# 28 of the 32 up blocks of each squared-ReLU layer as 14 pairs, each pair in seven products of half width

## The chip, the cores and the metric

The kernel runs on one core of a Trainium2 chip. The metric is the device time of one execution in microseconds, as the median of several runs. The engines of the core are PE (matrix products; its weight loads have a line of their own, PEld), DVE and ACT (elementwise work), POOL (elementwise work and transfers of its own queue) and SP (which issues most transfers). Each works through its own queue in order, and they wait for each other on semaphores.

## The reference

A transformer of two blocks on 512 tokens of 1024 features, in float32. First block: stick-breaking attention, a squared-ReLU layer, retention, a second squared-ReLU layer. Second block: a SwiGLU layer, a mixed attention and mLSTM layer, another SwiGLU layer. The change touches the two squared-ReLU layers:

```
def squared_relu_mlp(h, w_up, w_down):      # w_up 1024 x 4096, w_down 4096 x 1024
    u = jax.nn.relu(h @ w_up)
    return (u * u) @ w_down

h = h + squared_relu_mlp(rms_norm(h, g_mlp[layer]), w_mlp_up[layer], w_mlp_down[layer])
```

## The kernel before

Features lie on the 128 partitions and the T = 512 tokens along them. A product of full precision is built of three products of a shorter type (`fp32r`): with w = w_hi + w_lo and x = x_hi + x_lo it sums w_hi·x_hi, w_hi·x_lo and w_lo·x_hi in PSUM. A **block** is 128 output features from 1024 input features: `dense` (lines 2051 to 2065) issues 3 x 8 = 24 matmuls of 512 columns, each with its weight load.

Around every block there is the same small production line, two blocks ahead of PE: SP loads 512 KB of weights into `raw` (L466), ACT rounds them to `w_hi` (L578, 128x1024), DVE takes the rest as `w_lo` (L1197). Both halves have two slots.

A squared-ReLU layer has 32 up blocks and 32 down blocks, in groups of 8 (`groups`, one copy for each engine). The order is ups of group 0, ups of group 1, downs of group 0, ups of group 2, downs of group 1, and so on, so that 8 ups lie between the making of a group's hidden values and their use; `u_hi` and `u_lo` have two buffers for that. After an up block DVE forms relu(product) times the norm's reciprocal `inv` (L1209, `u_act`), ACT squares it (L757) and rounds it (L745, `u_hi`), DVE takes the rest (L1427, `u_lo`). After a down block DVE adds the product to the residual `h` in one operation (L1377). The ups' and downs' repetitions are loops on each engine (L206).

At a norm (`ahead_of_norm`, `residual_of_norm`, `of_new_x`) each chunk of the residual is added by DVE, rounded to `x_hi` by ACT (L593) and its rest `x_lo` taken by DVE (L1224), while POOL adds up squares (L2019, L2022); PE starts the next block chunk by chunk (L2099, L2102).

## Time and profile before

| | before |
|---|---|
| median of 3 runs | 2479.38 us (2479.18 to 2479.76) |
| profiled execution, span from first to last instruction | 2477.6 us |
| PE busy | 2469.6 us, 100% |
| DVE busy | 1384.1 us, 56% |
| ACT busy | 952.4 us, 38% |
| POOL busy | 104.0 us, 4% |
| DMA engines | 29.5% of their time, 91 GB/s on average |
| granted clock of PE | 1.00 throughout |

Times inside the kernel are microseconds from the span's start. A matmul's own duration in a row overlaps that of its neighbours; what a matmul costs in a stream is the distance between starts. The idle time in brackets behind a row is that of its engine just before it, with what ended it.

### The profile page before, as it was taken

The page shows a single profiled execution, that of the slowest core. Times are in us where ns is not written, and L with a number is a line of the kernel's source. Part 1 is how long each engine was busy: PE and PEld are TensorE (multiplying, and loading weights), DVE is VectorE, ACT ScalarE, POOL GpSimd, SP SyncE. Part 2 cuts the span into 40 slices and gives each one's busy share as a digit, 9 for nine tenths or more (in the row PEclk, how much of TensorE's full clock was granted, in tenths as well). Part 3 has the DMA queues.
Part 4 walks back from the last instruction along what each step waited for, and adds up shares of the span by engine and source line. Part 5 has one row for each costly group of instructions (what it writes and reads, how often), then busy time and mean ns, then how long its engine had stood idle before and what let it go on. Part 6 is the DMA issues. An engine that isn't in the chain of part 4 may idle for free.

```text
span 2477.6 us, 31594 instructions
## 1 busy us (share of the span) xinstructions
PE 2469.6 (100%) x11544; PEld 2029.9 (82%) x11544; DVE 1384.1 (56%) x1762; ACT 952.4 (38%) x1213; POOL 104.0 (4%) x83
## 2 busy tenths in 40 slices
PE   9999999999999999999999999999999999999999
PEld 7888888888888888888888888888777778888887
DVE  5777544344767765544344544545868846544343
ACT  3676433233334343442233323223465453333222
POOL 2000100001000000100002100001000001000000
PEclk9999999999999999999999999999999999999999
DMA  4112332233222222333333232333222223333333
GB/s 140 57 52 60 94 101 93 96 109 109 85 85 77 77 85 85 104 98 93 101 94 95 93 101 93 98 98 110 85 69 69 77 64 98 93 97 98 93 101 111
DMA packets 76061, 225.40 MB, mean 91 GB/s; under 512 B 12240, under 2 KB 22736, under 8 KB 75856
## 3 DMA queue, kind: packets, MB, share of 16 engines
q1 hardware_dynamic: 71744, 222.24, 29.5%
q10 hardware_dynamic: 4240, 2.10, 0.3%
q8 instruction: 52, 0.85, 0.1%
q14 instruction: 25, 0.20, 0.0%
HBM read 222.21 MB, written 2.10 MB: 91 GB/s over the span
## 4 chain that ended last, share of the span: by engine, by line
PE 97%; DVE 2%; issue 0%; DMA 0%; ACT 0%; ACTq 0%; SPq 0%; DVEq 0%
PE ps L2060 54%; PE ps L2065 27%; PE ps L2667 2%; PE ps L2129 2%; PE ps L2113 1%; PE ps L2410 1%; PE ps L2285 1%; PE ps L2242 1%; PE ps L2261 1%; PE ps L2226 1%; PE ps L2397 1%; PE ps L2248 1%; DVE score L1799 1%; PE ps L2644 0%; PE ps L2722 0%; PE ps L2274 0%
## 5 line engine op out<-in xcount | busy, mean ns | idle before, releaser
L578 ACT ACTIVATE w_hi<-raw 128x1024 fp32r<-128x1024 f32 x406 | 430.7, 1061 | 1204.0 <-PE ps L2065 1155.1
L2060 PE MATMUL ps<-x_hi,w_hi 128*128 128x512 f32 x1936 | 761.7, 393 | 0.0
L2060 PE MATMUL ps<-x_lo,w_hi 128*128 128x512 f32 x1936 | 754.0, 389 | 0.0
L1197 DVE TENSOR_TENSOR w_lo<-raw,w_hi 128x1024 fp32r<-128x1024 f32 x406 | 499.8, 1231 | 150.3 <-ACT w_hi L578 150.0
L2065 PE MATMUL ps<-x_hi,w_lo 128*128 128x512 f32 x1936 | 478.2, 389 | 0.0
L2060 PEld LDWEIGHTS ps<-x_hi,w_hi 128*128 128x128 f32 x1936 | 363.5, 188 | 80.6 <-issue 4.0
L2060 PEld LDWEIGHTS ps<-x_lo,w_hi 128*128 128x128 f32 x1936 | 363.6, 188 | 75.5 <-issue 1.7
L2065 PEld LDWEIGHTS ps<-x_hi,w_lo 128*128 128x128 f32 x1936 | 363.4, 188 | 75.6
L2060 PE MATMUL ps<-u_hi,w_hi 128*128 128x512 f32 x858 | 334.3, 390 | 0.0
L2060 PE MATMUL ps<-u_lo,w_hi 128*128 128x512 f32 x858 | 333.9, 389 | 0.0
L1377 DVE SCALAR_TENSOR_TENSOR h<-ps,h 128x512 f32 (+1 forms) x135 | 93.3, 691 | 337.6 <-PE ps L2065 333.3
L2065 PE MATMUL ps<-u_hi,w_lo 128*128 128x512 f32 x858 | 212.5, 389 | 0.0
L2065 PEld LDWEIGHTS ps<-u_hi,w_lo 128*128 128x128 f32 x858 | 161.0, 188 | 33.5
L2060 PEld LDWEIGHTS ps<-u_hi,w_hi 128*128 128x128 f32 x858 | 161.1, 188 | 33.4
L2060 PEld LDWEIGHTS ps<-u_lo,w_hi 128*128 128x128 f32 x858 | 161.0, 188 | 33.3
L1209 DVE SCALAR_TENSOR_TENSOR u_act<-ps,inv 128x512 f32<-128x512 f32 x108 | 74.6, 691 | 168.4 <-PE ps L2065 168.2
L1427 DVE TENSOR_TENSOR u_lo<-u,u_hi 128x512 f32 (+1 forms) x108 | 74.8, 693 | 59.0 <-ACT u_hi L745 59.0
L745 ACT ACTIVATE u_hi<-u 128x512 f32 (+1 forms) x108 | 68.3, 633 | 95.8 <-DVE u L1459 87.5
L1209 DVE SCALAR_TENSOR_TENSOR u<-ps,inv 128x512 f32<-128x512 f32 x44 | 30.4, 691 | 130.7 <-PE ps L2065 130.7
L2022 POOL TENSOR_TENSOR rstd<-rstd,xn 128x512 f32<-128x512 f32 x49 | 81.2, 1657 | 137.1 <-ACT xn L599 118.4
L2019 POOL COPY rstd<-xn 128x512 f32<-128x512 f32 x7 | 4.8, 688 | 1694.4 <-ACT xn L599 1384.7
L1224 DVE SCALAR_TENSOR_TENSOR x_lo<-h,prm,x_hi 128x512 fp32r<-128x512 f32 x48 | 48.5, 1018 | 4.4 <-ACT x_hi L593 4.2
(386 smaller groups left out, 2438.7 us busy)
## 6 DMA issues: line engine op xcount, KB each, us to landing
raw<-in_stream SPq DMA_DIRECT2D x413, 512.0 KB, 3.6
x_tok<-in_x SPq DMA_DIRECT2D x4, 512.0 KB, 7.8
out_x<-xn ACTq DMA_DIRECT2D x7, 256.0 KB, 2.3
tab_ret<-in_tables_ret SPq DMA_DIRECT2D x1, 1536.0 KB, 6.5
raw<-in_stream SPq DMA_DIRECT2D x3, 256.0 KB, 3.2
tab_mix<-in_tables_mix SPq DMA_DIRECT2D x1, 384.0 KB, 4.2
prm<-in_params SPq DMA_DIRECT2D x1, 298.5 KB, 4.7
out_x<-xn ACTq DMA_DIRECT2D x2, 128.0 KB, 1.8
```

The source lines that it names most:

```text
L578: nc.scalar.activation(w_hi[:, slot(n)], raw[:, slot(n)], ACT.Copy).then_inc(hi_done, 1)
L745: nc.scalar.activation(flat(u_hi[:, group % 2, at(t, scale, plus)]), u[:, plus], ACT.Copy).then_inc(sig("uh_done"), 1)
L1197: nc.vector.tensor_tensor(w_lo[:, slot(n)], raw[:, slot(n)], w_hi[:, slot(n)].bitcast(F32), ALU.subtract).then_inc(lo_done, 1)
L1209: nc.vector.scalar_tensor_tensor(out=dst, in0=product(n), scalar=scale, in1=inv[:], op0=op, op1=ALU.mult).then_inc(bank_free[slot(n)], 1)
L1224: nc.vector.scalar_tensor_tensor(out=x_lo[:, c], in0=h[:, c], scalar=gain, in1=x_hi[:, c].bitcast(F32), op0=ALU.mult, op1=ALU.subtract).th ...
L1377: nc.vector.scalar_tensor_tensor(out=dst, in0=product(n), scalar=scale, in1=dst, op0=ALU.mult, op1=ALU.add).then_inc(bank_free[slot(n)], 1)
L1427: nc.vector.tensor_tensor(flat(u_lo[:, group % 2, at(t, scale, plus)]), u[:, plus], flat(u_hi[:, group % 2, at(t, scale, plus)]).bitcast(F32),
L2022: nc.gpsimd.tensor_tensor(total[:], total[:], square, ALU.add).then_inc(sig("sum_done"), 1)
L2060: nc.tensor.matmul(ps[:, gemm_bank(n)], w_hi[:, s, k], x(k), start=(k == 0 and i == 0), stop=False)
L2065: last = nc.tensor.matmul(ps[:, gemm_bank(n)], w_lo[:, s, k], hi(k), start=False, stop=(k == kc - 1))
L2129: return nc.tensor.matmul(ps[:, VALUE_BANKS[g][tb]], x[:, c, tb * P:(tb + 1) * P], w[:, slot(n), PAIRS * k:PAIRS * (k + 1)].rearrange("p i ...
L2667: last = nc.tensor.matmul(ps[:, bank], w[:, slot(n), 4 * half + k], x[:, k], start=(k == 0 and i == 0), stop=(k == 3 and i == 2))
```

## The change

Four up blocks of each layer stay as they were. The other 28 are taken as 14 pairs. For a pair, the 256 x 1024 weights are a 2 x 2 arrangement of quarters (128 outputs x 512 inputs) and the input is a 2 x 2 arrangement (512 features x 256 tokens). In place of 8 quarter products, 7 products are computed, of sums of quarters on both sides (Winograd's form of Strassen's scheme, by which several products add up in one PSUM bank). One product, called a unit, is 12 matmuls of 256 columns: 4 chunks by 3 terms. A pair has 84 of them, where it had 48 of 512 columns.

New work around it. The sums of inputs (`xs_hi`, `xs_lo`) are made once for each layer at its norm. Of the weights, five of the seven forms lie in `forms`, which has two buffers, one for each pair in turn: SP loads three transfers (512, 512 and 256 KB) and POOL then issues a transfer of 512 KB that adds to what lies there; DVE adds up the other two (`form_sum`). ACT rounds each form (`form_high`), DVE takes the rest (`form_low`), in rings of four. The sums of products are read out of PSUM in halves: ACT copies two (`first_copy`, `second_copy`) between two units that add to the same bank, DVE one (`third_copy`), and DVE forms three sums. ACT then does relu, square and rounding as separate operations. The layer's norm factor is left out of the up blocks; its square `inv_sq` multiplies the down products, which thus take DVE two operations (`down_product`).

The order of the layer changes as well: 4 dense blocks and pairs 0 and 1, downs of group 0, pairs 2 to 5, downs of group 1, and so on. Each group's downs follow directly on its own ups, and the hidden values have one buffer, since the forms take the place of the other.

In the diff, `load_forms` is SP's, `add_forms` POOL's, the first loop over `v` ACT's, the second DVE's and `of_new_u` PE's.

```diff
+def up_phase(layer, g):
...
+    units = [(qs[0], p) for p in (1, 2, 6, 5, 7)]
+    for q in qs[1:]:
+        units += [(q, 1), (q - 1, 4), (q - 1, 3), (q, 2), (q, 6), (q, 5), (q, 7)]
+    return units + [(qs[-1], 4), (qs[-1], 3)]
...
+            def load_forms(q):
...
+                if q % UP_PAIRS < 2:
+                    sp.wait_ge(mm_done, RUN_AT[("mlp0", "mlp1")[q // UP_PAIRS]] + 2 + 1)
+                else:
+                    sp.wait_ge(*upto("f_lo", UNIT_AT[q - 2, 3] + 1))
+                into = forms[q % 2]
+                sp.dma_start(into[:, 0:2].rearrange("p a f -> p (a f)"), stream[block]).then_inc(flag(f"r_in_{q % 2}"), 16)
+                sp.dma_start(into[:, 3:5].rearrange("p a f -> p (a f)"), stream[block + 1]).then_inc(flag(f"r_in_{q % 2}"), 16)
+                sp.dma_start(into[:, 2], stream[block, :, 0:T]).then_inc(flag(f"r_in_{q % 2}"), 16)
...
+            def add_forms(q):
...
+                pool.wait_ge(*upto(f"r_in_{q % 2}", 48 * (q // 2 + 1)))
+                nc.gpsimd.dma_start(forms[q % 2][:, 2:4].rearrange("p a f -> p (a f)"), stream[up_block_at(q) + 1],
+                                    accum_op=ALU.add).then_inc(sig(f"added_{q % 2}"), 16)
...
+                for v in range(first, first + len(units)):
...
+                    if before and before[1] in (1, 6):
+                        copy_of(*before)
+                    if v + 3 < end:
+                        form_high(v + 3)
+                    if q > qs[0] and p == 6:
+                        squared(q - 1, 0)
...
+                for v in range(first, first + len(units)):
...
+                    if before[1] == 7:
+                        fourth_sum(layer, before[0])
...
+                    if p == 4 and q + 1 < (layer + 1) * UP_PAIRS:
+                        third_form(q + 1)
+                    if v + 2 < end:
+                        form_low(v + 2)
+                    if p == 3 and q + 1 < (layer + 1) * UP_PAIRS:
+                        fourth_form(q + 1)
+                    if p == 4 and q > qs[0]:
+                        up_low(layer, q - 1, 0)
+                    if p == 7 and q > qs[0] + 1:
+                        up_low(layer, q - 2, 1)
+                if len(qs) > 1:
+                    up_low(layer, qs[-2], 1)
+                third_sum(qs[-1])
+                up_low(layer, qs[-1], 0)
+                up_low(layer, qs[-1], 1)
...
+            def of_new_u(n, made):
...
+                for chunks in (range(KC - 2), (KC - 2,), (KC - 1,)):
+                    pe.wait_ge(sig("ul_done"), made + chunks[-1] + 1)
```

On PE, at the end of a group's ups and the start of the downs that follow, the queue of before reads (loop bodies; `ul_done` counts the hidden chunks that are ready):

```order
L2065 MATMUL ps<-x_hi,w_lo 128x512 [waits lo_done]
L2065 MATMUL ps<-x_hi,w_lo 128x512 x7
L206 REGISTER_ALU
L206 COMPARE_AND_BRANCH
L206 UNCONDITIONAL_BRANCH [waits ul_done]
L206 ISA
L2051 REGISTER_ALU [waits hi_done]
L2060 MATMUL ps<-u_hi,w_hi 128x512 [waits bank_free_0]
```

And now (`sph_done` and `spl_done` count the rounded forms and their rests, `su_done` DVE's operations on products):

```order
L2820 MATMUL ps<-xs_hi,ring 128x256 [waits su_done,sph_done]
...
L2824 MATMUL ps<-xs_hi,ring_b 128x256 [waits spl_done]
L2824 MATMUL ps<-xs_hi,ring_b 128x256 x3
L2837 MATMUL ps<-u_hi,w_hi 128x512 [waits lo_done,ul_done,bank_free_0,hi_done]
L2837 MATMUL ps<-u_hi,w_hi 128x512 x5
L2837 MATMUL ps<-u_lo,w_hi 128x512 x6
L2837 MATMUL ps<-u_hi,w_lo 128x512 x6
L2837 MATMUL ps<-u_hi,w_hi 128x512 [waits ul_done]
```

The downs now wait for chunks of the units just before them, the first 18 matmuls for chunks 0 to 5 together; before, they waited for chunks made 8 blocks earlier.

On DVE, at the end of a group's ups, the queue of before is this loop body and then the downs':

```order
L1209 SCALAR_TENSOR_TENSOR u_act<-ps,inv 128x512 [waits mm_done]
L1197 TENSOR_TENSOR w_lo<-raw,w_hi 128x1024 [waits hi_done]
L1426 REGISTER_ALU
L1427 ISA [waits uh_done]
L1427 TENSOR_TENSOR u_lo<-u,u_hi 128x512
L206 REGISTER_ALU
L206 COMPARE_AND_BRANCH
L206 UNCONDITIONAL_BRANCH
L206 ISA
L1377 ISA [waits mm_done]
L1377 SCALAR_TENSOR_TENSOR h<-ps,h 128x512
```

And now, from the end of unit 7 of the group's last pair (`third_copy` is `fourth_sum`'s first half, L1740 and L1745 are the third and fourth form of the next group's first pair, `added_0` the adding transfer, L1783 the hidden values' rests):

```order
L1768 COPY third_copy<-ps 128x256 [waits cum_done,su_done]
L1770 TENSOR_TENSOR u<-ps,third_copy 128x256 [waits cum_done,su_done]
L1740 TENSOR_TENSOR form_sum<-forms_80 128x512 [waits x_in_2,added_0]
L1733 TENSOR_TENSOR ring_b<-forms_80,ring 128x512 [waits sph_done]
L1783 TENSOR_TENSOR u_lo<-u_act,u_hi 128x512 [waits uh_done]
L1733 TENSOR_TENSOR ring_b<-forms_80,ring 128x512 [waits sph_done]
L1745 TENSOR_TENSOR form_sum<-forms_80,form_sum 128x512 [waits sp_done]
L1783 TENSOR_TENSOR u_lo<-inv_final,u_hi 128x512 [waits uh_done]
L1776 TENSOR_TENSOR u<-ps,second_copy 128x256 [waits cum_done,exp_done]
L1783 TENSOR_TENSOR u_lo<-u,u_hi 128x512 [waits uh_done] x2
L1681 TENSOR_TENSOR down<-ps,inv_sq 128x512 [waits mm_done,qkl_done]
```

The rest of chunk 5 (the second L1783 row), for which PE's first down matmul waits, now stands behind four operations on the next pair's weights, one of which waits for a transfer.

On ACT, in the middle of a group, the queue had for each up block these rows:

```order
L578 ACTIVATE w_hi<-raw 128x1024 [waits mm_done]
L757 ACTIVATE u<-u_act 128x512 [waits bank_free_0]
L744 REGISTER_ALU
L745 ISA [waits u_done]
L745 ACTIVATE u_hi<-u 128x512
```

And now, where the next pair but one is first read (`x_in_2` counts SP's three transfers into `forms`, buffer 0):

```order
L911 ACTIVATE ring<-forms_81 128x512 [waits cum_done,added_1] x2
L938 ACTIVATE u_act<-u_act 128x256 [waits su_done]
L911 ACTIVATE ring<-forms_80 128x512 [waits cum_done,x_in_2]
L946 ACTIVATE u_act<-u_act 128x512 [waits ln_done]
L918 ACTIVATE second_copy<-ps 128x256 [waits su_done,cum_done]
L911 ACTIVATE ring<-form_sum 128x512 [waits cum_done,sp_done]
```

`second_copy`, for which PE's unit 7 waits, now stands two places behind the row that waits for SP's transfers.

## Rows read from the trace of the kernel before

**Rows 1.** Page, parts 1 and 4: busy time of each engine; the chain that ended last.

```profile
PE 2469.6 (100%) x11544; PEld 2029.9 (82%) x11544; DVE 1384.1 (56%) x1762; ACT 952.4 (38%) x1213; POOL 104.0 (4%) x83
...
PE 97%; DVE 2%; issue 0%; DMA 0%; ACT 0%; ACTq 0%; SPq 0%; DVEq 0%
```

**Rows 2.** Timeline, DVE, in the ups: start, duration, engine, line, operation.

```profile
306.14 0.69 DVE L1209 SCALAR_TENSOR_TENSOR u_act<-ps,inv 128x512 f32<-128x512 f32 x1 [2.26 <-PE ps L2065]
...
349.66 0.69 DVE L1209 SCALAR_TENSOR_TENSOR u_act<-ps,inv 128x512 f32<-128x512 f32 x1 [2.20 <-PE ps L2065]
```

**Rows 3.** Timeline, PE, 256-column matmuls of the last block, second and eighteenth.

```profile
2469.00 0.28 PE L2743 MATMUL ps<-u_lo,w_hi 128*128 128x256 f32 x1
...
2470.91 0.28 PE L2743 MATMUL ps<-u_hi,w_lo 128*128 128x256 f32 x1
```

**Rows 4.** Timeline, PE: the last up block of group 1, then downs.

```profile
353.31 1.75 PE L2065 MATMUL ps<-x_hi,w_lo 128*128 128x512 f32 x7
354.90 0.39 PE L2060 MATMUL ps<-u_hi,w_hi 128*128 128x512 f32 x1
```

**Rows 5.** Groups by form, DVE and ACT: count, busy us, mean ns, idle before.

```profile
L1427 DVE TENSOR_TENSOR u_lo<-u,u_hi 128x512 f32 x102 | 70.6, 693 | 54.3 <-ACT u_hi L745 54.3
...
L757 ACT ACTIVATE u<-u_act 128x512 f32<-128x512 f32 x64 | 39.5, 617 | 9.9 <-DVE u_act L1209 9.9
...
L745 ACT ACTIVATE u_hi<-u 128x512 fp32r<-128x512 f32 x6 | 3.8, 632 | 3.9 <-DVE u L1459 3.8
...
L1163 ACT ACTIVATE xn<-ps 128x256 f32<-128x256 f32 x2 | 0.8, 384 | 2.2 <-PE ps L2113 2.2
```

**Rows 6.** One line's instructions, DVE on 256 columns of PSUM: min/median/max ns.

```profile
L1394 DVE SCALAR_TENSOR_TENSOR h<-ps,h x2: 425/425/425, 2471.2 to 2473.8; 128x256 f32<-128x256 f32 x2
```

**Rows 7.** Timeline: a product's last matmuls, the next block's first, DVE's answer.

```profile
320.44 1.98 PE L2065 MATMUL ps<-x_hi,w_lo 128*128 128x512 f32 x8
322.26 0.39 PE L2060 MATMUL ps<-x_hi,w_hi 128*128 128x512 f32 x1
...
322.46 0.69 DVE L1209 SCALAR_TENSOR_TENSOR u_act<-ps,inv 128x512 f32<-128x512 f32 x1 [2.23 <-PE ps L2065]
```

**Rows 8.** DMA issues: count, KB each, median us from issue to landing.

```profile
raw<-in_stream SPq DMA_DIRECT2D x413, 512.0 KB, 3.6
x_tok<-in_x SPq DMA_DIRECT2D x4, 512.0 KB, 7.8
...
tab_ret<-in_tables_ret SPq DMA_DIRECT2D x1, 1536.0 KB, 6.5
```

**Rows 9.** DMA view of the first 20 us in 40 slices: GB/s.

```profile
GB/s 0 0 0 41 119 119 346 342 281 198 250 295 193 297 387 385 387 385 379 385 387 383 389 301 301 352 385 394 349 352 74 29 0 33 0 0 0 0 55 164
```

**Rows 10.** Timeline: the last chunk of the norm behind the first layer.

```profile
616.94 0.72 ACT L593 ACTIVATE x_hi<-h,prm 128x512 fp32r<-128x512 f32 x1 [3.91 <-DVE h L1377]
...
618.96 0.39 PE L2099 MATMUL ps<-x_hi,w_hi 128*128 128x512 f32 x1
```

**Rows 11.** Timeline, DVE, while POOL computes, and after it.

```profile
242.70 1.72 DVE L1197 TENSOR_TENSOR w_lo<-raw,w_hi 128x1024 fp32r<-128x1024 f32 x1
...
246.75 1.23 DVE L1197 TENSOR_TENSOR w_lo<-raw,w_hi 128x1024 fp32r<-128x1024 f32 x1
```

More of the change, by code:

```diff
@@ new lines, in load_mlp @@
+            def load_mlp(layer, first, extra=None):
+                load_run(first, first + UP_DENSE)
+                for i in range(2):
+                    load_forms(layer * UP_PAIRS + i)
+                load(first + UP_DENSE)
+                load(first + UP_DENSE + 1)
+                for g in range(len(MLP_GROUPS)):
+                    qs = sorted({q for q, _ in up_phase(layer, g)})
+                    for q in qs:
+                        if q + 2 < (layer + 1) * UP_PAIRS:
+                            load_forms(q + 2)
+                    n = first + UP_DENSE + DC * g + 2
+                    if g + 1 < len(MLP_GROUPS):
+                        load_run(n, n + DC - 2)
+                        load(n + DC - 2)
+                        load(n + DC - 1)
+                    else:
+                        if extra is not None:
+                            extra()
+                        load_run(n, n + DC - 2)
@@ L746, in hidden_hi, with form_high @@
                                      ACT.Copy).then_inc(sig("uh_done"), 1)
-            def mlp(first, chunks_before, norm, next_norm):
-                def up(n, t, group, before):
-                    for i in range(2):
-                        split_hi(later(n, i + 2))
-                        if t is None and i == 0 and group == 0:
-                            root(norm)
-                        done = before + i + 1 if t is None else t * 2 + (before + i + 1)
-                        m = later(n, i)
-                        freed(m)
-                        nc.scalar.activation(u[:, i], u_act[:], ACT.Square).then_inc(sig("u_done"), 1)
-                        hidden_hi(t, 2, i, done, group)
-                groups(MLP_GROUPS, first, chunks_before, 1, up, next_norm)
+            def form_high(v):
+                q, p = UNITS[v]
+                if p in (5, 7):
+                    act.wait_ge(sig(f"added_{q % 2}"), 16 * (q // 2 + 1))
+                elif p in (6, 4):
+                    act.wait_ge(*upto("f_sum", 2 * q + (6, 4).index(p) + 1))
+                else:
+                    act.wait_ge(*upto(f"r_in_{q % 2}", 48 * (q // 2 + 1)))
+                if v >= FORM_SLOTS:
+                    act.wait_ge(*upto("f_mm", v - FORM_SLOTS + 1))
+                nc.scalar.activation(form_hi[v % FORM_SLOTS], form_of(q, p), ACT.Copy).then_inc(flag("f_hi"), 1)
@@ L1412, in residual_of_norm @@
                 sum_low(k)
+                if k in (N_MLP0, N_MLP1):
+                    x_forms_low(k, 1)
             def residual_of_final(first, scale):
@@ L1429, in hidden_lo, with form_low @@
                                         ALU.subtract).then_inc(sig("ul_done"), 1)
[L1431 to L1442 removed]
+            def form_low(v):
+                q, p = UNITS[v]
+                dve.wait_ge(*upto("f_hi", v + 1))
+                nc.vector.tensor_tensor(form_lo[v % FORM_SLOTS], form_of(q, p), form_hi[v % FORM_SLOTS].bitcast(F32),
+                                        ALU.subtract).then_inc(flag("f_lo"), 1)
@@ new lines, in of_new_u @@
+            def of_new_u(n, made):
+                pe.wait_ge(hi_done, number(n, 1))
+                bank_is_free(n)
+                pe.wait_ge(lo_done, number(n, 3))
+                for chunks in (range(KC - 2), (KC - 2,), (KC - 1,)):
+                    pe.wait_ge(sig("ul_done"), made + chunks[-1] + 1)
+                    for i, (w, x) in enumerate(((w_hi, u_hi), (w_hi, u_lo), (w_lo, u_hi))):
+                        for k in chunks:
+                            last = nc.tensor.matmul(ps[:, gemm_bank(n)], w[:, slot(n), k], x[:, 0, k],
+                                                    start=(k == 0 and i == 0), stop=(k == KC - 1 and i == 2))
+                last.then_inc(mm_done, 1)
@@ new lines, in mlp @@
+            def mlp(layer, first, norm):
+                of_new_x(first, norm)
+                for i in range(1, UP_DENSE):
+                    of_x(first + i, (lambda: mean_square(norm)) if i == 1 else None)
+                n = first + UP_DENSE
+                pe.wait_ge(sig("std_done"), norm_turn(norm))
+                for g in range(len(MLP_GROUPS)):
+                    for unit in up_phase(layer, g):
+                        up_unit(UNIT_AT[unit])
+                    of_new_u(n, layer * HIDDEN // P + KC * g)
+                    dense(n + 1, lambda k: u_hi[:, 0, k], lambda k: u_lo[:, 0, k])
+                    run(n + 2, DC - 2, lambda k: u_hi[:, 0, k], lambda k: u_lo[:, 0, k])
+                    n += DC
```

383 lines of the change are left out of this document (342 added, 41 removed).

## The prediction

> **What bounds the kernel now.** The page's first part and the chain that ended last come first [rows 1]: PE is busy for 2469.6 of 2477.6 us and makes up 97% of the chain. DVE and ACT are half idle. So a matmul's time taken away is a gain, as long as nobody else becomes late; and any wait that PE gets is a loss in full. Next, the pace. DVE's reads of the up products stand at 306.14 and, eight blocks later, 349.66 [rows 2]: 43.52 / 8 = 5.44 us for a block of 24 matmuls, 226.7 ns each. From ups to downs PE does not pause: the row of seven matmuls that starts at 353.31 is followed at 354.90 by the first down matmul, 7 x 0.227 later [rows 4]. The ends of groups cost nothing today.
>
> **The gain on PE.** Sixteen gaps between 256-column matmuls last 2470.91 - 2469.00 = 1.91 us, 119.4 ns each [rows 3], a little more than half of 226.7. A unit is 12 x 0.1194 = 1.433 us, a pair 7 of them, 10.03 us, against 2 x 5.44 = 10.88. That is 0.85 us for a pair and 23.8 us for 28, in place of the 38 us that one product in eight would be at equal cost per column.
>
> The Trainium skill ("TensorE: Matmul & The Clock Gate", Back-to-back issue gap) has 262 cycles for 256 columns and 518 for 512 at 2.4 GHz, 109 and 216 ns. The rows have 119 and 227. By the page the gain would be 1.2 us a pair, 33 us; I stay with the rows.
>
> **Do the other two keep up?** For each pair DVE has seven rests of forms, two form sums and two rests of hidden values, 11 operations on 512 columns at 0.69 [rows 5], and four on 256 columns of PSUM at 0.425 [rows 6]: 9.3 us. ACT has seven roundings and two more of hidden values at 0.63, two squares and a relu at 0.62, three reads of 256 columns at 0.38 [rows 5], and a relu of 256 that I put at 0.40: 9.1 us. Both fit into 10.03, with under 1 us to spare. So in the pairs a wait of either that is longer than what it is ahead of PE reaches PE. Where an engine waits for PE it answers 0.20 us after PE has gone on to its next work (322.26 to 322.46) [rows 7].
>
> **Wait 1, in the middle of a group.** Only two buffers of forms exist. Those of a group's first two pairs are loaded under the downs before; those of its third and fourth are loaded among the units. Count from the start of unit 1 of pair q-1 on PE. DVE reads pair q-2's unit 7 out at 0.20 (0.85 us), and takes the rest of its last form (0.69): at 1.74 the buffer is free and SP issues 1280 KB for pair q. ACT wants them in the iteration of unit 6; behind that rounding (0.63) stand a square (0.62) and `second_copy` (0.38), for which PE's unit 7 waits, due at 6 x 1.433 = 8.60. The rounding must therefore start at 6.92, and the transfers have 5.2 us. A load of 512 KB takes 3.6 and one of 1536 KB 6.5 [rows 8]; between them 1280 KB take 5.8. PE waits 0.65 us. Two pairs of each group with four, three such groups in a layer, two layers: 12 x 0.65 = 7.8 us.
>
> **Wait 2, at the end of a group.** PE's first down matmul needs chunk 5, whose rest stands on DVE behind the next group's weights. From the end of unit 7 of the last pair, DVE runs: 0.20, two operations on 256 columns 0.85, third form, rest, rest of chunk 4, rest, fourth form, rest of chunk 5, six at 0.69: done at 5.2. PE in that time waits for `third_copy` (0.20 + 0.42 + 0.05) since unit 4 follows unit 7 directly and adds to the same bank, then does two units (2.87): 3.54. So PE stands for 0.67 + 1.7 = 2.4 us even when no transfer is late. The chunks 6 and 7 are ready before PE has done 18 matmuls of 512 columns (4.1 us).
>
> The third form, however, waits for POOL's adding transfer. Its buffer was freed one pair earlier, and DVE comes to it 9.3 us after that. The chain L is SP's transfers, 5.8, and then the adding one. **No row shows such a transfer.** From below it is bounded by a plain 512 KB, 3.6; from above by 7.8, the median of four 512 KB loads that were in flight with others [rows 8]. I take it as moving its bytes twice, since it reads what it adds to: 3.6 plus another 512 KB at (6.5 - 3.6) / 2 = 1.45, about 5.0. L is then 10.9 with 0.1 for two hand-overs, DVE is held for 1.6, and PE stands 4.0 us. Six groups have a next one: 24 us. (In the middle of a group the same wait is hidden: DVE has 1.9 us of lead there, which covers L up to 12.5.)
>
> The last group of each layer has no next pair. There 0.67 for the copy and about 0.5 for chunk 5 remain: 2.4 us for both layers.
>
> The Trainium skill ("Collectives: The Full Stack", The bandwidth ceiling) says of adding in the transfer path that the add itself costs nothing but two source reads halve the rate. No row can show it here; it is the same doubling that I took from bytes.
>
> **The rest.** At a norm behind such a layer the residual costs two operations instead of one. The last `x_hi` is ready at 617.66 and PE wants it at 618.96 [rows 10]; 1.3 us of cover take the extra 0.7. The sums of inputs add some 3 us of DVE work for each of the last chunks ahead of the layer, where DVE has about 2 to spare: 0 to 1 us a layer, I take 1 for both. The split of 28 weight blocks on ACT and DVE, the multiplication by `inv` and the reciprocal that DVE had to finish first all go, but from engines with half their time idle: nothing. POOL computes nothing in the pairs; only while it did was DVE slowed (1.72 instead of 1.23) [rows 11], and should descriptor writing do the same, DVE's spare is gone.
>
> **The sum.** -23.8 + 7.8 + 24.0 + 2.4 + 1.0 = +11.4 us. Made against the profiled span of 2477.6, which lies 1.8 below the median, it carries over unchanged: 2479.4 + 11.4 = **2491 us**, half a percent slower. With the adding transfer at 3.6, L is 9.5 and the ends cost 2.5 each: 2482. With 7.8, L is 13.7, the ends cost 6.8 (41 us), and the wait in the middle passes its cover by 1.2 us in 6 to 12 places: 2516.
>
> **Rivals.**
> *The transfers come in time (faster).* If 1280 KB land within 5.2 us and both steps within 9.3, neither wait exists. The start of the kernel speaks for it, where the queues move 385 GB/s once they are full [rows 9]: 1280 KB at that rate are 3.4 us plus the 2.2 us that a single 512 KB load shows beyond its own 1.4. That is 5.6, still over 5.2, and two such fixed parts are in L. Then the sum is -23.8 + 6 x 2.4 + 2.4 = -7: 2472. It decides at L = 9.3; each microsecond above it costs 6.
> The Trainium skill ("DMA: Bandwidth & Descriptors", Anatomy of one DMA) fits a DMA as 2.0 us plus bytes / 436 GB/s, so 5.0 and 3.2 us here. By that page L is 8.3 and this rival is the result. The rows contradict it for plain loads (3.6 against 3.2 for 512 KB).
> *The adding transfer is slow.* Nothing in the trace excludes 8 us or more. Every microsecond above my 5.0 costs 6 us, and above L = 12.5 up to twice that: 2505 to 2530.
> *The units don't run at 119 ns.* Each has two to four waits where a block of twice its matmuls has three, and two engines above 90%. At 125 ns a pair costs 10.5, most of the gain is gone, and the time is 2504. For it speaks the small spare; against it that the 18 matmuls of [rows 3] and blocks with waits run without a gap.
>
> **How the numbers follow.** My forecast, with both waits there and the adding transfer between 3.6 and 7 us (2482 to 2504): 0.50, of which 0.06 below 2484. Transfers in time or nearly (2468 to 2484): 0.30, of which 0.21 below 2474. Slow adding transfer (2505 to 2530): 0.12. Units slower, or DVE and ACT behind (2495 to 2520): 0.08. About 0.2% is what a measurement can tell here, 5 us: faster 0.21, same 0.15, slower 0.64. The range 2471 to 2517 leaves out the ends of both sides.
>
> **What would show it.** Right, if PE's rows in a unit stand 0.119 apart; if PE's idle time is almost all in front of the first down matmul (six times about 3 to 4 us, on `u_lo`) and of unit 7 (on ACT's copy); if DVE's third form waits for a DMA at each group's end. Wrong, if that form waits for nothing (then time is below 2480), if the transfers on POOL's queue take far from 5 us, or if PE waits in every pair for a form's rest, which would make DVE the bound.

## The result: 2.6% slower, and the profile after

The changed kernel takes 2543.2 us (median of 4, 2542.0 to 2546.6), the kernel before in the same comparison 2479.5: a ratio of 1.026, 95% interval 1.0245 to 1.0274. The forecast was 2491, with a range from 2471 to 2517. The direction was right, the size was not: 64 us are lost, not 11, and the time lies outside the range. Times below are medians of executions in the faster of the chip's two states; one execution of the run without input sums fell in the slower one (2573.2 us, clock 0.915) and is left out.

The page of the changed kernel, to be read beside [rows 1]: busy time of each engine, the chain that ended last, and the issues of the forms' transfers (count, KB, median us to landing).

```profile
PE 2474.6 (97%) x12552; PEld 2075.5 (82%) x12552; DVE 1532.9 (60%) x2120; ACT 1073.1 (42%) x1517; POOL 125.8 (5%) x111
...
PE 85%; DVE 5%; DMA 4%; issue 2%; ACT 2%; POOL 1%; SPq 0%; DVEq 0%; ACTq 0%; POOLq 0%
...
forms<-in_stream SPq DMA_DIRECT2D x56, 512.0 KB, 4.5
forms<-in_stream POOLq DMA_DIRECT2D x28, 512.0 KB, 5.5
forms<-in_stream SPq DMA_DIRECT2D x28, 256.0 KB, 5.5
```

PE has 1008 matmuls more, since those of the pairs have 256 columns instead of 512, and is busy for longer than before, in a span of 2544.7 us instead of 2477.6. Its share of the chain falls from 97 to 85%. Two things are new: PE waits, and in part of its busy time it is slow. The timeline of PE shows both (start, duration, operation, and in brackets the idle time ahead and what ended it).

```profile
273.44 0.79 PE L2516 MATMUL ps<-x_hi,w_hi 128*128 128x512 f32 x1 [3.90 <-ACT x_hi L723]
...
301.58 0.55 PE L2820 MATMUL ps<-x_hi,ring 128*128 128x256 f32 x1 [5.63 <-ACT ring L911]
301.93 0.41 PE L2820 MATMUL ps<-x_lo,ring 128*128 128x256 f32 x1
302.14 0.41 PE L2820 MATMUL ps<-x_hi,ring 128*128 128x256 f32 x1
...
307.01 0.28 PE L2820 MATMUL ps<-xs_lo,ring 128*128 128x256 f32 x1
307.13 0.28 PE L2820 MATMUL ps<-xs_hi,ring 128*128 128x256 f32 x1
...
320.80 0.64 PE L2824 MATMUL ps<-xs_hi,ring_b 128*128 128x256 f32 x4
322.11 0.36 PE L2820 MATMUL ps<-x_hi,ring 128*128 128x256 f32 x1 [0.68 <-DVE third_copy L1768]
...
331.92 2.90 PE L2837 MATMUL ps<-u_hi,w_hi 128*128 128x512 f32 x6 [6.70 <-DVE u_lo L1783]
...
396.15 0.36 PE L2820 MATMUL ps<-xs_hi,ring 128*128 128x256 f32 x1 [1.93 <-ACT second_copy L918]
```

Matmuls of 256 columns start 0.12 us apart at 307, and 0.213 apart at 302, behind an idle of 5.63 us. All idle time of PE in the two layers, added up from its brackets:

| PE waits for | places | us |
|---|---|---|
| `x_hi` of the norm's last chunk | 2 | 7.8 |
| the first unit's form, start of a layer | 2 | 11.3 |
| `third_copy`, end of a group | 8 | 5.6 |
| `u_lo`, first down matmul | 8 (6.70, 2.92, 6.12, 0.38; 2.62, 6.29, 2.63, 0.38) | 28.0 |
| `second_copy` | 8 (0.20 to 1.93) | 7.2 |
| other | | 1.3 |

Together 61 us. The rest is seen in the granted clock. The table of stretches, in the changed kernel: stretch and its length, busy time of PE, PE's weight loads, DVE, ACT and POOL, the granted clock, the share and GB/s of DMA.

```profile
326.00:341.00 15.00, 9.08 (x28) 7.28 (x29) 5.90 (x10) 5.26 (x9) 0.86 (x1) 0.66 0.53 154
...
516.00:531.00 15.00, 10.54 (x36) 8.53 (x37) 7.62 (x12) 5.67 (x9) 0.86 (x1) 0.77 0.46 139
...
1304.00:1315.00 11.00, 10.35 (x46) 8.59 (x47) 4.65 (x7) 3.27 (x5) 0.86 (x1) 1.00 0.58 159
```

In nine places, all behind an idle of 2.6 to 6.7 us, the clock is at its lower level, 1.2 of 2.4 GHz, for 3 to 6 us of work; behind the 2.63 us that end at 1304.65 it is not. What the starts of matmuls lie further apart there than 0.120 and 0.227 us sums to 21 us over the nine. The kernel before never fell below 1.00 in these layers. The Trainium skill ("TensorE: Matmul & The Clock Gate", Why this matters for your kernels) warns of idle gaps between bursts of matmuls for this reason, and here the trace agrees. Its rule for the lower level (Part 1, columns / 1.2 GHz from start to start) gives 213 ns for 256 columns, which is what the rows at 302 show.

The balance of the spans: -22.4 (28 pairs x (10.88 - 10.08)) + 61 + 21 = +59.6, and 67.1 were measured. Some 5 of the missing 7.5 us lie in how the brackets count. A bracket begins at the end of the matmul before it, 0.28 or 0.39 us behind its start, where the next one could have started after 0.12 or 0.227. The last of the four matmuls from 320.80 starts at 321.16, and the next at 322.11: 0.95 us, of which 0.12 is the pace, so the wait of 0.68 costs 0.83. At some 30 waits that is 0.16 us each. About 2 us more are delays under 0.11 us, mostly at starts of units.

### The profile page after: what moved, and what is told of

It is laid out like the page before. It is cut to its first block, busy times and chain, and to the rows that moved or that the text cites. A ratio compares the mean times of both kernels' runs of the same rounds, so it can differ in the third digit from the quotient of the medians.

```text
span 2544.7 us, 33902 instructions
## 1 busy us (share of the span) xinstructions
PE 2474.6 (97%) x12552; PEld 2075.5 (82%) x12552; DVE 1532.9 (60%) x2120; ACT 1073.1 (42%) x1517; POOL 125.8 (5%) x111
## 4 chain that ended last, share of the span: by engine, by line
PE 85%; DVE 5%; DMA 4%; issue 2%; ACT 2%; POOL 1%; SPq 0%; DVEq 0%; ACTq 0%; POOLq 0%
PE ps L2477 41%; PE ps L2482 20%; PE ps L2820 4%; DMA forms<-in_stream 4%; PE ps L2824 2%; PE ps L2837 2%; PE ps L3146 2%; PE ps L2546 2%; PE ps L2889 1%; PE ps L2530 1%; PE ps L2701 1%; PE ps L2658 1%; PE ps L2677 1%; PE ps L2642 1%; PE ps L2876 1%
## 5 line engine op out<-in xcount | busy, mean ns | idle before, releaser
L2477 PE MATMUL ps<-x_hi,w_hi 128*128 128x512 f32 x1488 | 588.0, 395 | 0.0
L2477 PE MATMUL ps<-x_lo,w_hi 128*128 128x512 f32 x1488 | 580.3, 390 | 0.0
L2482 PE MATMUL ps<-x_hi,w_lo 128*128 128x512 f32 x1488 | 367.6, 389 | 0.0
L2477 PEld LDWEIGHTS ps<-x_lo,w_hi 128*128 128x128 f32 x1488 | 280.1, 188 | 58.3 <-issue 1.7
L2482 PEld LDWEIGHTS ps<-x_hi,w_lo 128*128 128x128 f32 x1488 | 279.3, 188 | 58.1
L2820 PE MATMUL ps<-xs_hi,ring 128*128 128x256 f32 x448 | 113.2, 285 | 7.5 <-ACT second_copy L918 7.2
L2820 PE MATMUL ps<-xs_lo,ring 128*128 128x256 f32 x448 | 112.2, 283 | 0.0
L911 ACT ACTIVATE ring<-forms 128x512 fp32r<-128x512 f32 x140 | 87.4, 626 | 50.3 <-PE ps L2824 30.2
L2820 PE MATMUL ps<-x_hi,ring 128*128 128x256 f32 x336 | 87.6, 292 | 16.9 <-ACT ring L911 11.3
L2820 PEld LDWEIGHTS ps<-xs_hi,ring 128*128 128x128 f32 x448 | 86.1, 192 | 9.5 <-ACT ring L911 7.3
```

Of the source, the lines that this page charges most:

```text
L911: nc.scalar.activation(form_hi[v % FORM_SLOTS], form_of(q, p), ACT.Copy).then_inc(flag("f_hi"), 1)
L2477: nc.tensor.matmul(ps[:, gemm_bank(n)], w_hi[:, s, k], x(k), start=(k == 0 and i == 0), stop=False)
L2482: last = nc.tensor.matmul(ps[:, gemm_bank(n)], w_lo[:, s, k], hi(k), start=False, stop=(k == kc - 1))
L2820: nc.tensor.matmul(bank, form_hi[s][:, j * P:(j + 1) * P], x_part(p, j, i == 0), start=(p in (1, 2, 5) and j == 0 and i == 0), stop=False, ...
```

## Experiments

Each is an edit of the changed kernel; times are medians. Waits of PE are from the same brackets as above.

### The order at a group's end

DVE's part (ACT's third rounding moves in the same way):

```diff
+                    late = q == qs[-1] and p in (4, 3)
-                    if p == 4 and q + 1 < (layer + 1) * UP_PAIRS:
+                    if p == 4 and q + 1 < (layer + 1) * UP_PAIRS and not late:
                         third_form(q + 1)
...
                 up_low(layer, qs[-1], 1)
+                if v + 1 < end:
+                    third_form(qs[-1] + 1)
+                    fourth_form(qs[-1] + 1)
+                    form_low(v + 1)
+                    form_low(v + 2)
```

> At a group's end the next group's third and fourth form, its first two rests (DVE) and its third rounding (ACT) are issued behind the rest of chunk 7 instead of ahead of those of chunks 5 to 7. Everything is computed. Theory (PE waits there because u_lo of chunk 5 stands on DVE behind a form that waits for the adding transfer, and what PE idles there also lowers its clock): the eight waits in front of the first down matmul fall from 28.0 us in all to the 0.4 each that the last group of a layer has today, 3 us; the half-clock stretches behind them go too, some 10 us; time about 2543 - 25 - 10 = 2508. Rival 1 (the idle is not DVE's order but its load, so it moves on to the next group's first units): time within 8 us of 2543, PE then waits in front of the first units of groups 1 to 3. Rival 2 (only the idle counts, the clock costs nothing): 2518.

Measured: 2507.8 us (ratio 1.0118, 1.0101 to 1.0135). The timeline around the first group's end: the issues of the pair's first load and of its adding transfer, and DVE, both in the changed kernel; then DVE and PE with the new order.

```profile
312.91 0.33 SPq L639 DMA_DIRECT2D forms<-in_stream  x1
...
320.02 0.86 POOL L2435 DMA_DIRECT2D forms<-in_stream  x1 [29.50 <-DMA forms<-in_stream]
```

```profile
322.00 0.42 DVE L1770 TENSOR_TENSOR u<-ps,third_copy 128x256 f32<-128x256 f32 x1
328.07 0.69 DVE L1740 TENSOR_TENSOR form_sum<-forms 128x512 f32<-128x512 f32 x1 [5.65 <-DMA forms<-in_stream]
328.68 0.68 DVE L1733 TENSOR_TENSOR ring_b<-forms,ring 128x512 fp32r<-128x512 f32 x1
329.28 0.69 DVE L1783 TENSOR_TENSOR u_lo<-u_act,u_hi 128x512 fp32r<-128x512 f32 x1
...
331.09 0.68 DVE L1783 TENSOR_TENSOR u_lo<-inv_final,u_hi 128x512 fp32r<-128x512 f32 x1
```

```profile
323.61 0.69 DVE L1785 TENSOR_TENSOR u_lo<-inv_final,u_hi 128x512 fp32r<-128x512 f32 x1 [1.74 <-ACT u_hi L954]
...
327.69 0.68 DVE L1742 TENSOR_TENSOR form_sum<-forms 128x512 f32<-128x512 f32 x1
```

```profile
324.44 0.93 PE L2845 MATMUL ps<-u_hi,w_hi 128*128 128x512 f32 x3 [0.37 <-DVE u_lo L1785]
```

All eight waits for `u_lo` are 0.37 or 0.38 us, 3.0 in all. The third form now waits for nothing, and 35 us come back, as the theory had it. Both rivals fall: the idle did not move on, and idle alone does not make up the gain. Between the two profiled executions, 39.5 us apart, the waits in the layers fall from 61 to 34 us (25 of it for `u_lo`), and what is lost at the lower clock falls by another 12.

### Transfers without their bytes

```diff
+                if q % UP_PAIRS >= 2:
+                    for i in range(3):
+                        sp.dma_start(into[:, i, 0:16], stream[block, :, 0:16]).then_inc(flag(f"r_in_{q % 2}"), 16)
+                    return
```

> Transfers of forms for the third pair of a layer and all behind it are cut to 16 columns each, on SP's and on POOL's queue; their number, order and waits stay. What they would bring is left out, so those products are of old forms. Theory (late transfers make second_copy's waits whole, and most of u_lo's; the order of DVE's work alone leaves about 1.7 us in front of the first down matmul at six ends, as I worked out for a transfer in time): second_copy's 7.2 us go, u_lo's 28.0 fall to 6 x 1.7 + 2 x 0.4 = 11, and since 1.7 us is too short to lower the clock, 10 more: 2543 - 7 - 17 - 10 = 2509. Rival (DVE's order, not the transfer, holds u_lo): u_lo stays above 20 us and the time above 2525.

Measured: 2501.2 us, 8 below what I expected. The waits for `second_copy` are gone. Those for `u_lo` are 0.96 us at the six ends and 0.38 at the last ones, 6.6 in all, less than the 11 I expected. DVE at the first end, in the forecast's own order, without a late transfer:

```profile
320.76 0.68 DVE L1744 TENSOR_TENSOR form_sum<-forms 128x512 f32<-128x512 f32 x1
321.36 0.68 DVE L1737 TENSOR_TENSOR ring_b<-forms,ring 128x512 fp32r<-128x512 f32 x1
321.96 0.68 DVE L1787 TENSOR_TENSOR u_lo<-u_act,u_hi 128x512 fp32r<-128x512 f32 x1
```

Durations of 0.68 stand 0.60 apart: one operation begins before the one ahead of it has ended. I had stacked them at 0.69. So with the transfers in time the first down matmul waits 0.96 us an end and not 1.7 (0.6 of it is the order, since 0.38 stays where no pair follows); the rest of `u_lo`'s wait is the transfers.

At the first end they take longer than I had put them: the first load of the pair is issued at 312.91, the adding transfer at 320.02, and the form starts at 328.07. That is 15.2 us where I had 10.9: 7.1 for SP's 1280 KB (5.8) and 8.1 for the adding one (5.0). But the six ends of the changed kernel are of two kinds. At three, 11.0 to 11.3 us pass from the first issue to the landing of the adding transfer, which itself takes 5.2 to 5.5; PE waits 2.62 to 2.92 us for `u_lo`. At the other three it is 14.5 to 15.1 us, with 7.7 to 8.0 for the adding transfer, and PE waits 6.12 to 6.70. At these the next pair's forms are issued 0.2 to 0.5 us behind the adding transfer (320.25 here, with two weight blocks behind them), at the others 1.5 to 1.7 us behind it. That this is why it takes longer is likely, but no run moved that load alone.

### second_copy ahead of the next pair's rounding

```diff
+                    if before and before[1] == 6 and v + 2 < end:
+                        form_high(v + 2)
-                    if v + 3 < end:
+                    if p != 6 and v + 3 < end:
                         form_high(v + 3)
```

> ACT's rounding of the next pair's first form, which waits for SP's loads, is issued behind second_copy instead of ahead of it. Everything is computed. Theory (wait 1 of the prediction is this rounding): the eight waits in front of unit 7, 7.2 us in all in the changed kernel, fall under 1 us; no half-clock stretch follows them, so nothing more: 2543 - 7 = 2536. Rival (the rounding, then later, makes the next pair's unit 1 late instead): 2541 or more, with PE waiting for form_hi or form_lo in front of unit 1.

Measured: 2533.3 us (2528.1 to 2542.0). ACT in the changed kernel, where PE's 1.93 us at 396.15 come from:

```profile
394.58 0.63 ACT L911 ACTIVATE ring<-forms 128x512 fp32r<-128x512 f32 x1 [3.64 <-DMA forms<-in_stream]
...
395.64 0.36 ACT L918 ACTIVATE second_copy<-ps 128x256 f32<-128x256 f32 x1
```

With the edit PE's waits for `second_copy` are gone but for one of 0.13 us. Three waits for a form in front of unit 4 at group ends are new (0.85, 1.31, 1.30), since the edit also moved the last pair's own rounding. Wait 1 thus stands where the forecast had it. Its size agrees only as a sum (7.2 against my 7.8): there were not twelve waits of 0.65 us but eight from 0.20 to 1.93, since the 1280 KB landed after 5.3 to 7.3 us at the twelve places. That the time fell by 10 and not 7 is within what this version's times scatter.

### Is the clock a loss of its own?

```diff
                 pe.wait_ge(lo_done, number(n, 3))
+                for i in range(FILL[n]):
+                    nc.tensor.matmul(ps[:, gemm_bank(n)], w_hi[:, slot(n), i % KC], x_hi[:, i % KC], start=True, stop=True)
```

> In front of the wait for u_lo of chunk 5 PE does matmuls of 512 columns on data that is there, 24, 8, 22 and 0 of them in the four groups of the first layer and 7, 22, 7 and 0 in the second, into the bank that the down block then starts anew. They take 0.227 us each at full clock, 20.4 us in all, less than the idle that stood there. Everything is computed. Theory (idle of over about 2.6 us is followed by matmuls at half the clock, which cost 10 us behind these waits): the granted clock stays at 1.00 around 326 to 336, 425 to 428, 517 to 524, 1118 to 1121 and 1210 to 1217 us, and the time is 2543 - 10 = 2533. Rival (the low granted clock is only a record of the idle; the loss is the waits): within 3 us of 2543.

Measured: 2537.6 us, 5.6 less than the changed kernel, with useless work added and nothing that PE waits for made earlier. The same kind of stretches, around the first down matmul of a group (their places in the span have moved), the first and the third, and the first of the second layer:

```profile
324.00:339.00 15.00, 14.14 (x62) 11.37 (x61) 7.85 (x12) 5.69 (x9) 0.86 (x1) 1.00 0.57 163
...
501.00:516.00 15.00, 14.29 (x83) 12.50 (x82) 7.47 (x13) 7.98 (x15) 1.73 (x2) 1.00 0.83 227
1107.00:1118.00 11.00, 9.33 (x34) 7.54 (x35) 4.98 (x9) 4.32 (x7) 0.86 (x1) 0.84 0.54 150
```

At four of the six ends the clock stays at 1.00. At the two others PE had 1.6 us of fillers and then still idled 1.88 and 2.24 us, and the clock fell (0.84). The clock is thus a cost of its own, and the rival falls; but only half of the gain I expected came. In the traces, what is lost at the lower clock falls by some 11 us; part of it is taken back by the waits for `second_copy`, 10.1 us in this run where they were 7.2. When it falls isn't told by the length of the idle alone: 2.63 us at 1304 left it at 1.00 in the changed kernel, and 1.88 did not here.

### The start of a layer: three causes in a row

The first run leaves the input sums out in effect; the second also puts the roundings of forms ahead of a weight block's.

> The sums of inputs are left out in effect: each of their instructions on ACT and DVE works on 16 columns instead of 256 to 1024, and the units read plain x instead of the sums. PE does the same matmuls. Theory (the sums hold DVE and ACT up in the norm and the dense up blocks, which I had put at 1 us for both layers): the waits of 3.9 us for the last x_hi and of 5.6 us for the first unit go in both layers, 19 us, and with them four half-clock stretches, about 10 us: 2543 - 19 - 10 = 2514. Rival 1 (the residual in two operations with its scaling, not the sums, delays the norm): the 3.9 stay in the second layer (1065), where such a residual stands ahead, and the time is 2522 or more. Rival 2 (loading of forms from layer start is late for the first unit): the 5.6 stay, 2530.

> The sums of inputs are left out in effect, as in the run without them, and the first three roundings of forms are issued ahead of the rounding of the second down block's weights. In the run without sums PE still waited 4.35 and 4.17 us for the first unit, while ACT stood 3.7 us for that block's load. Theory (that load, queued behind 2.5 MB of forms, is the second cause): these two waits fall under 0.8 each, with two half-clock stretches, some 4 us: 2520 - 7 - 4 = 2509. Rival (the load of the forms themselves is late): the waits stay above 2, now with ACT waiting for forms: 2515 to 2520.

```diff
                 for c in range(UP_DENSE):
-                    split_hi(first + c + 2)
+                    if c < 3:
+                        split_hi(first + c + 2)
...
                             form_high(v)
+                        split_hi(first + c + 2)
                     freed(first + c)
```

Measured: 2516.4 (2514.7 to 2523.2) and 2516.1 us (2514.3 to 2519.4). Without the sums both waits for the last `x_hi` are gone, so that part is theirs; the residual in two operations (rival 1) has no share. In the changed kernel ACT and DVE wait for each other there; ACT, then DVE:

```profile
270.49 1.33 ACT L870 ACTIVATE x_fp<-h,prm 128x512 f32<-128x512 f32 x2 [4.75 <-DVE x_sum L1670]
271.73 1.04 ACT L877 ACTIVATE xs_hi<-x_sum 128x1024 fp32r<-128x1024 f32 x1
272.68 0.71 ACT L723 ACTIVATE x_hi<-h,prm 128x512 fp32r<-128x512 f32 x1
```

```profile
270.03 0.42 DVE L1670 TENSOR_TENSOR x_sum<-x_sum,x_fp 128x256 f32<-128x256 f32 x1
270.38 0.68 DVE L1635 SCALAR_TENSOR_TENSOR h<-ps,h 128x512 f32<-128x512 f32 x1
```

`x_fp` has one buffer, so ACT stands 4.75 us for a sum on DVE, and its two scaled inputs and the rounding of a sum lie between that and the last `x_hi`, for which PE waits 3.90. DVE is idle for 40% of the span and yet late here, because each of the two stands in program order behind the other.

In front of the first unit, in the changed kernel, it is again DVE that ACT waits for. DVE's reciprocal, then ACT:

```profile
284.00 3.35 DVE L1490 RECIPROCAL inv<-std 128x512 f32<-128x512 f32 x1 [3.09 <-ACT std L761]
```

```profile
290.25 1.34 ACT L870 ACTIVATE x_fp<-h,prm 128x512 f32<-128x512 f32 x2 [4.02 <-DVE x_sum L1670]
...
300.80 1.15 ACT L911 ACTIVATE ring<-forms 128x512 fp32r<-128x512 f32 x2 [0.35 <-DVE xs_lo L1676]
```

DVE stands 3.09 us for the square root and then spends 3.35 on the reciprocal, with the sums and the dense blocks' work behind it. No run moved the reciprocal alone, so its share isn't known.

The first unit's wait did not go with the sums (4.35 and 4.17 us are left). ACT in the run without sums, and the two transfers issued from 283.5 to 284.4 (KB, us to landing):

```profile
291.54 1.06 ACT L708 ACTIVATE w_hi<-raw 128x1024 fp32r<-128x1024 f32 x1 [3.74 <-DMA raw<-in_stream]
292.50 1.14 ACT L911 ACTIVATE ring<-forms 128x512 fp32r<-128x512 f32 x2
```

```profile
forms<-in_stream POOLq DMA_DIRECT2D x1, 512.0 KB, 8.1
raw<-in_stream SPq DMA_DIRECT2D x1, 512.0 KB, 7.5
```

ACT stands for a weight block of the downs, and the first roundings are behind it. My words for that load, "queued behind 2.5 MB of forms", are not what the trace shows: it was issued at 283.99, when DVE's rest of an earlier block had freed its place; SP's forms had landed by 283.3, and it flew beside an adding transfer. With the roundings ahead, 0.85 + 1.19 and 0.40 + 2.42 are left, so the waits fall by 3.7 us and not by 8.5, and the time does not fall at all (2516.4 and 2516.1). The number is the rival's (2515 to 2520), but its reason isn't seen: in the ups' last blocks ACT waits for DVE and for weights, not for forms. In the changed kernel, where the sums come first, ACT waits 0.35 us for DVE and not for this load; as a cause there it is not shown.

Next, with the sums computed, an order that spreads them: fewer in the norm, one in each dense block, the square root a block later, and the reciprocal behind the first group's pairs (it is wanted only by the downs).

```diff
-                    if k in (N_MLP0, N_MLP1) and c >= 6:
+                    if k in (N_MLP0, N_MLP1) and c == 6:
                         x_forms_low(k, c - 6)
...
                     up_pairs(layer, g)
+                    if g == 0:
+                        inverse(norm)
+                        nc.vector.tensor_tensor(inv_sq[:], inv[:], inv[:], ALU.mult).then_inc(flag("down_scaled"), 2)
```

> Only the work ahead of the units is put in another order, in both layers; everything is computed. In the norm one sum of inputs is made among the chunks, the second behind the last; the rest of each is made in the next dense block; the square root is issued one block later; reciprocal and inv_sq move behind the first group's pairs; the first three roundings of forms are issued ahead of the rounding of a down block's weights, which waits for its load behind 2.5 MB of forms. Theory (three causes in a row: sums, reciprocal on DVE, that load): the waits for the last x_hi (3.9, twice) fall under 0.5 and those for the first unit (5.6, twice) under 1.5, and four half-clock stretches go: 2543 - 17 - 10 = 2516, down to 2512. Rival (DVE is simply full from the norm's last chunks to the first unit, in whatever order): at least half of the 19 us of waits stays, 2528 or more.

Measured: 2527.2 us. The norm's waits are gone, the first unit's 5.67 and 5.27 us stay: more than half of the 19, so the rival is nearer in number. Its reason (DVE full) is not what the trace shows. I took this order together with that of the ends:

> Three changes of order together, everything computed: that of the group ends, that of the start of the layer, and that of second_copy (the next pair's first rounding behind it in the middle of a group, and all three roundings of the next group behind the last up_high). Theory (idle of PE and its clock are all that stands between the pairs' gain of 22 us and the time): of 61 us of waits about 5.6 (third_copy) + 3.0 (u_lo) + 3 stay, no stretch at half clock: 2479.4 - 22.4 + 11.6 + 3 = 2472, faster than the kernel before by 0.3%. Rival (the orders only move the waits, since DVE and ACT have 0.7 and 0.9 us to spare in a pair): 2485 or more.

Measured: 2490.1 us (1.0044, 1.003 to 1.0058), where the rival had put 2485 or more; but the orders did more than move the waits. Of 61 us 22 are left, 11 of them in front of the first units. DVE in that run, and what ACT did meanwhile:

```profile
287.15 0.69 DVE L1846 TENSOR_TENSOR u_lo<-u,u_hi 128x512 fp32r<-128x512 f32 x1 [3.81 <-ACT u_hi L1019]
```

```profile
281.64 1.06 ACT L877 ACTIVATE xs_hi<-x_sum 128x1024 fp32r<-128x1024 f32 x1 [1.46 <-DVE x_sum L1680]
282.61 1.32 ACT L870 ACTIVATE x_fp<-h,prm 128x512 f32<-128x512 f32 x2
283.95 1.28 ACT L761 ACT_TABLE_LOAD   x1
285.25 0.69 ACT L761 ACTIVATE std<-ps,eps 128x512 f32<-128x512 f32 x1
```

My own new order had put five operations of ACT, a table load among them, ahead of a rounding that DVE stood for. So it was mended:

```diff
+                    if c < 3:
+                        x_forms_high(norm, c + 1)
+                    if c in (0, 1):
+                        x_scaled(norm, c + 2)
+                    if c == 1:
+                        root(norm)
```

(now behind each block's `u_hi`, and with the buffers of forms numbered so that the first two do not lie over the sums' inputs)

> As the run with all three orders, everything computed, with the start of the layer put in order once more: in each dense block ACT does the square and its rounding first, then the sum's rounding and the scaled inputs for the next sum, and the square root behind those of the second block; DVE's first two rests of forms stand ahead of the two form sums; and the forms' buffers are numbered so that the first two units' do not lie over the inputs of the sums. Theory (the 5.67 and 5.27 us in front of the first unit are a chain in which ACT and DVE wait in turn, 3.8 us for u_hi and 2.6 us for x_sum in the trace, and not work that fills either): those waits fall under 1 us each and their half-clock stretches go, 9.5 + 4: 2490 - 13 = 2477. Rival (DVE is full there; 3 sums of 2.6 us with 4 blocks of 2.5 us and forms of 2.6): at least 3 us a layer stay, 2483 or more.

Measured: 2483.9 us (1.0019, 1.001 to 1.0028). The first unit waits 0.33 and 0.24 us, but 3.03 and 3.04 us stand in front of the third unit, whose rounding is behind the fourth dense block's work. ACT there:

```profile
293.19 0.63 ACT L1009 ACTIVATE u<-u_act 128x512 f32<-128x512 f32 x1 [2.44 <-DVE u_act L1843]
```

So at least 3 us a layer stayed, and the time is the rival's (2483 or more). DVE works without a pause from 288.79 to 294.28 here: for this stretch and in this order it is full. The clock's mean is 1.000 in the profiled execution.

### The last waits

> As the run with the start in order again, everything computed; in a group's last pair the units come as 1, 6, 2, 7, 5, 4, 3 (with the pair before's 4 and 3 behind 1) instead of 1, 2, 6, 5, 7, 4, 3, so that unit 5 lies between unit 7 and unit 4 and covers DVE's read of third_copy. Theory (the eight waits of 0.7 us for third_copy, and half of those of 0.38 for u_lo, are order): 5.6 us less, and nothing on the clock: about 2471, faster than the kernel before by 0.3%. Rival (the sixth unit's form, now a unit earlier, comes late behind POOL's adding transfer): PE waits for form_hi or form_lo in front of unit 6 in at least 6 places, and the time stays at or above that of the run it builds on.

Measured: 2487.0 us, 3 more than the run it builds on. The waits for `third_copy` are gone, and six for `first_copy` (0.64 to 1.83, 7.0 in all) stand in their place. The rival names the cause (unit 6's form is late) but not the way: PE does not wait for that form, it waits for what ACT does behind it.

```profile
388.80 0.63 ACT L914 ACTIVATE ring<-form_sum 128x512 fp32r<-128x512 f32 x1 [3.20 <-DVE form_sum L1752]
...
389.86 0.36 ACT L921 ACTIVATE first_copy<-ps 128x256 f32<-128x256 f32 x1
```

```diff
+                    if before == (qs[-1], 1) and qs[-1] > qs[0]:
+                        form_high(v + 2)
...
+                        form_high(layer * len(UNITS) // 2 + 2)
+                        copy_of(layer * UP_PAIRS, 1)
+                        form_high(layer * len(UNITS) // 2 + 3)
                         split_hi(first + c + 2)
```

> As the run with the units in another order, everything computed, with two more moves. In a group's last pair ACT issues the rounding of unit 6's form, which waits for POOL's adding transfer, behind first_copy instead of ahead of it. At the start of a layer the rests and roundings of the first four forms and the first first_copy stand ahead of what is left of the fourth dense block. Theory (the six waits for first_copy, 7.0 us in all, and the two of 3.0 for the third unit are order): all but 1.5 us of them go, 11.5 less: profiled span 2484 - 11.5 = 2472, time about 2475, faster than the kernel before by 0.2%. Rival (the adding transfer itself is late there, or the fourth dense block's work, now later, makes chunk 5 late at the first group's end): PE waits for form_hi in front of unit 6, or 2 us and more for u_lo at the first end, and the time stays at 2480 or more.

Measured: 2476.3 us (median of 11, 2474.5 to 2478.1) against 2479.1: a ratio of 0.9988, 0.9979 to 0.9997. The waits for `first_copy` at the group ends are gone. In part the rival holds: PE waits 0.92 and 0.88 us for unit 6's form at two ends, and 4.2 us are left around the first units of both layers (6.8 two runs earlier). The page:

```profile
PE 2454.1 (99%) x12552; PEld 2059.2 (83%) x12552; DVE 1532.7 (62%) x2120; ACT 1071.6 (43%) x1517; POOL 126.2 (5%) x111
```

PE is busy 15.5 us less than in [rows 1] and idle for 12.7 us in the layers. The change with its work in another order is 67 us faster than as it was made, and by 0.1% faster than the kernel before; the interval only just leaves out no gain.

## Why the prediction was wrong

In the order of its sum:

- **The gain on PE: right.** A unit takes 1.44 us, a pair 10.08: -22.4 against -23.8. The rival by which units don't run at 119 ns is out.
- **Wait 1: right**, 7.2 against 7.8 us, at the instruction I named, shown by the run that moved it. That the sums agree so well is in part luck: the single waits ran from nothing to 1.93 us.
- **Wait 2 and the last groups: the mechanism right, the terms off.** 33.6 us against 26.4 for `third_copy` and `u_lo`. At three of the six ends L was 11.0 to 11.3, as forecast (10.9); at the other three it was 14.5 to 15.1, with 7.7 to 8.0 us for the adding transfer and not 5.0. I priced each transfer as if nothing else were loaded, and at those ends the next pair's forms are issued within half a microsecond of it. Against that the first down matmul waits 0.96 us with the transfers in time and not 1.7, for I stacked durations instead of start-to-start distances (0.60). The rival of the slow transfer was true at half of the ends, that of transfers in time at none. The Trainium skill's fit behind the latter ("DMA: Bandwidth & Descriptors", Anatomy of one DMA) is given there for transfers of POOL's queue; it makes 3.2 us of 512 KB, and the adding ones took 5.2 to 8.0.
- **"Nothing" for the reciprocal and the norms, "0 to 1 us a layer" for the input sums: this step failed.** It is 19.1 us (7.8 + 11.3). I compared DVE's spare time with the work added, and never laid out the order in which ACT and DVE wait for each other over a single buffer, nor saw that the reciprocal, which I had counted as gone, stays in front of the first unit. How the 11.3 us divide between reciprocal, sums and dense blocks stays open. Spare time said "fits", and with another order all but some 4 us do fit; the order as written did not. Four of the nine stretches at the lower clock follow these waits, so the step cost about 30 us and not 19.
- **The clock: a term that the sum lacked**, about 21 us. I costed each wait at its length. Idle of 2.6 us and more was mostly followed by matmuls at the lower level. The run that kept PE busy shows the effect, and the run of the group ends its size (12 us less lost at the lower clock, beside 28 us less of waits).
- **The rest**, some 7 us: 5 are the 0.16 us by which each wait costs more than its bracket, the others delays too short for a bracket. It is still there in the last version: -22.4 + 12.7 of idle would give 2467.9 as its span, and 2476.1 was measured; 30 waits at 0.16 are 5 of these 8.

Errors: +1.4 - 0.6 + 7.2 + 18.1 (19.1 less the 1.0 I had) + 21 + 7 and 1.3 of other waits are 55 us, and 67.1 - 11.4 = 55.7 had to be found. The rivals of the prediction stayed within two terms, the transfer and the pace of the units; the range could not hold what lay outside it. Had its bound taken the measured 15.2 for L, the ends would have read up to 50 us, too much, since only three of the six ends waited that long (6.1 to 6.7 us) and the others 2.6 to 2.9.

## What to carry to other kernels

A change that trims the bounding engine by a per cent turns every other engine's order into the question: for each new operation, write down what stands behind it on its engine and who waits for that, at the seams (norm, first block, end of a group) above all; a share of busy time of 60% says nothing there. A wait of PE of the size seen here should be priced at more than its length, since the matmuls behind it may run at half the clock. And try the order before giving up the change: here moves of order alone (and another numbering of buffers), none of arithmetic, took 2543 to 2476, though by no more than 0.1% past the kernel before.

## What the runs showed of the hardware

- Behind idle stretches of 2.6 to 6.7 us PE's granted clock was at 1.2 GHz for 3 to 6 us of work in nine of ten cases, and each of the nine cost 1.5 to 3 us on top of the idle. 3.03 and 3.04 us in a later version left it at 1.00, in the next one 3.04 us lowered it, and 1.88 us did behind a burst of fillers. With fillers that left less than 1.2 us of idle it stayed at 2.4 GHz.
- DVE's operations on 512 columns with durations of 0.68 us start 0.60 us apart when nothing is waited for.
- A transfer of 512 KB that adds to SBUF, on POOL's queue, takes 5.5 us in the median and up to 8.0 beside others; with 8 KB it took 2.4, and a plain one of 8 KB on SP's queue 1.7 (medians of the run with small loads). Issuing one costs POOL 0.86 us.
- The Trainium skill ("TensorE: Matmul & The Clock Gate", Back-to-back issue gap) gives 109 ns between matmuls of 256 columns at the full clock; the units here have 120, and [rows 3] 119. At the lower clock its figure and the trace agree.
